# A sparse expert stage whose down matrices are requested by ScalarE instead of SyncE

## The reference, cut to what matters

```
def swiglu(x, w_gu, w_down):
    gate, up = jnp.split(x @ w_gu, 2, axis=-1)
    return (jax.nn.silu(gate) * up) @ w_down
...
    def block(acc, inp):
        tok, wt, ex = inp
        y = swiglu(x_pad[tok], w_gu[ex], w_down[ex])
        return acc.at[tok].add((y * wt[:, None]).astype(acc.dtype)), None
```

## Time and profile before

| | |
|---|---|
| time, median of 3 executions | 2914.94 us (2910.91 to 2915.69) |
| span of the profiled execution | 2949.8 us |
| PE busy | 2637.6 us, 89% of the span |
| DVE, ACT, POOL busy | 762.9, 441.0, 493.7 us |
| expert stage | from about 1941 to 2903 us |
| weight requests of SP in the expert stage | 65 of 2048 KB and 65 of 1024 KB |

### The profile page before, as it was taken

One profiled execution on the slowest core, in us unless ns is written; L12 is line 12 of the kernel. 1 busy time (PEld: TensorE's weight loads), 2 busy tenths in 40 slices (PEclk: granted clock), 3 DMA queues, 4 the chain that ended last, 5 costly groups with the idle time before them and its releaser, 6 DMA issues. The chain is left out here.

```text
span 2949.8 us, 28375 instructions
## 1 busy us (share of the span) xinstructions
PE 2637.6 (89%) x11406; PEld 1618.1 (55%) x11406; DVE 762.9 (26%) x1394; ACT 441.0 (15%) x724; POOL 493.7 (17%) x449
## 2 busy tenths in 40 slices
PE   5999889999997999999994469959999999999992
PEld 3444444346994444444444124447777777778881
DVE  4011544654432111111233202211121211111114
ACT  1001113244541000000000000001111111111110
POOL 2000110111531000000010530012232333322221
PEclk9999999999998999999995779979999999999996
DMA  5011002100003111220104600089989999999984
GB/s 220 29 40 46 15 15 90 43 8 8 1 1 122 32 32 38 58 89 0 71 0 156 127 12 0 0 295 292 273 270 280 282 278 285 291 347 362 356 297 149
DMA packets 179592, 391.58 MB, mean 133 GB/s; under 512 B 14832, under 2 KB 53360, under 8 KB 178704
## 3 DMA queue, kind: packets, MB, share of 16 engines
q1 hardware_dynamic: 153616, 302.67, 30.3%
q0 software_dynamic: 24992, 80.21, 10.9%
q10 hardware_dynamic: 864, 7.02, 0.6%
HBM read 327.48 MB, written 62.39 MB: 132 GB/s over the span
## 5 line engine op out<-in xcount | busy, mean ns | idle before, releaser
L1888 PEld LDWEIGHTS banks<-arena 128*128 128x128 f32 x4160 | 531.3, 191 | 44.3 <-issue 43.1
L1888 PE MATMUL banks<-arena 128*128 128x128 f32 (+7 forms) x4160 | 540.0, 290 | 0.8 <-DVE arena L2046 0.8
L1298 PE MATMUL banks<-arena 128*128 128x512 f32 x768 | 341.0, 596 | 15.9 <-DMA arena<-in_w_branch 12.4
L363 PE MATMUL banks<-arena 128*128 128x512 f32 x640 | 279.2, 593 | 2.2 <-DVE arena L1021 1.9
L1835 POOL DMA_INDIRECT acc_scratch<-arena x100 | 154.5, 1545 | 634.5 <-DMA acc_scratch<-arena 340.5
L1298 PEld LDWEIGHTS banks<-arena 128*128 128x128 f32 x768 | 145.4, 190 | 204.6 <-issue 204.6
L1896 PE MATMUL banks<-arena 128*128 128x512 f32 (+1 forms) x536 | 244.5, 598 | 2.3 <-DVE arena L2048 0.9
L363 PEld LDWEIGHTS banks<-arena 128*128 128x128 f32 x640 | 119.4, 189 | 156.5 <-issue 148.6
L1304 PE MATMUL banks<-arena 128*128 128x512 f32 x384 | 172.7, 592 | 0.0
L356 PE MATMUL banks<-arena 128*128 128x512 f32 x384 | 167.2, 596 | 1.6 <-PEq L282 0.9
L1896 PEld LDWEIGHTS banks<-arena 128*128 128x128 f32 (+1 forms) x536 | 96.1, 189 | 101.8 <-issue 98.1
(11 more groups left out here) (342 smaller groups left out, 2514.8 us busy)
## 6 DMA issues: line engine op xcount, KB each, us to landing
arena<-in_exp_w_gu SPq DMA_DIRECT2D x65, 2048.0 KB
arena<-in_exp_w_down SPq DMA_DIRECT2D x65, 1024.0 KB
arena<-in_w_in SPq DMA_DIRECT2D x10, 2048.0 KB, 9.0
arena<-in_w_in SPq DMA_DIRECT2D x24, 512.0 KB, 5.9
arena<-in_w_branch SPq DMA_DIRECT2D x24, 256.0 KB, 6.1
arena<-in_x SPq DMA_DIRECT2D x4, 1024.0 KB
h_scratch<-arena SPq DMA_DIRECT2D x1, 4096.0 KB, 12.9
arena<-in_w_out SPq DMA_DIRECT2D x2, 2048.0 KB, 12.1
```

Source lines behind the costliest of these rows:

```text
L363: last = nc.tensor.matmul(PS[:, bank, :], wt[:, k, ct * P:(ct + 1) * P], hT[:, k, half * HALF:(half + 1) * HALF], start=(k == 0), stop=(k ...
L1298: last = nc.tensor.matmul(PS[:, b, :], wm[u][:, k, n, :], hT[:, k, hs], start=(k == 0), stop=(k == KD - 1))
L1888: last = nc.tensor.matmul(PS[:, bank + part, f * n:(f + 1) * n], weights[:, k, part * FF + f * P:part * FF + (f + 1) * P], by_k(x, n)[:, k ...
```

## The change

SP no longer requests the down matrices of the ranks. ACT does, in its own queue: four before anything else in the stage, the fifth after the spill loop, and that of rank r+5 at the end of its work on rank r. Each time it first loads the expert's number from the table. The gate/up matrices and the spill expert's two matrices stay with SP.

```
-                    if r >= RING:
-                        sp.wait_ge(x_dn, chunks(r - RING + 1))
-                    sp.dma_start(dn[r % RING], dn_v[bass.ds(e, 1)].rearrange("a p f n -> p (a f) n")).then_inc(x_wd[r % RING], 16)
...
+                def down_in(r):
+                    e = table(act, rank_e, r, NE - 1)
+                    if r >= RING:
+                        act.wait_ge(x_dn, chunks(r - RING + 1))
+                    act.dma_start(dn[r % RING], dn_v[bass.ds(e, 1)].rearrange("a p f n -> p (a f) n")).then_inc(x_wd[r % RING], 16)
+
+                for r in range(RING - 1):
+                    down_in(r)
                 act.wait_ge(x_xt, 1)
                 x_half(0, 0, P)
...
+                act.wait_ge(s_dn, n + 1)
+                act.nop(nofuse=True)
+                down_in(RING - 1)
                 for r in range(NE):
...
                     if more(r):
                         y_half(r, yoB, gateB, more(r), c + 1)
+                    if r + RING < NE:
+                        down_in(r + RING)
```

## The result

| | us |
|---|---|
| before, median of 5 executions | 2914.35 (2910.91 to 2915.69) |
| changed, median of 5 | 2924.63 (2921.76 to 2926.97) |
| ratio | 1.0039, 95% interval 1.0026 to 1.0051 |

The changed kernel is slower by 10.3 us in the medians (11.4 us by the ratio); the interval of the ratio is 7.6 to 14.9 us of 2914. One of the 23 executions of the kernel before on the chip of the last runs took 6534 us, where the others took 2945.5 to 2955.4, and is left out of their ratios.

The account below looks back on a forecast made before the run. PE was taken to bound the expert stage, except its entry, where DMA engines limit. Spill weights +9, scatter and gather -2, the rest 0: +7 us on 2914.94, 2922; own range 2917 to 2926, 8 in 10 2911 to 2933.

Parts of the forecast that it names:

- Steady cost 0: In the ranks: ACT's table load and request, 1.15 us each, hidden in its idle time; 0, bound 0 to 3 us.
- rival 4: ACT is held at its own requests at the entry, delaying its copy of the first rows: +5 to +15 us; chance 0.05.
- rival 3: Two-chunk ranks: a third busy queue lengthens POOL's scatters until its chain bounds the kernel, 25 us, 2940; chance 0.12.
- The delay of the spill weights: Stage entry: four down matrices, 4.19 MB, pass ahead of the spill expert's weights, delaying the spill block's matmuls 9 us.
- the bounds: Stage entry: spill-weight delay depending on how the two queues share, from 3.6 or 6.3 us to the full 10.7 us.
- What comes back: Behind the spill block: scatter and next gather meet an emptied queue and give back 2 us.
- the pair: Spill block's scatter plus the gather behind it: 16.2 us instead of 18.2, bounds 12.8 to 18.2.
- not 5 to 8: Sign in the changed profile: PE's idle for the gather behind the spill block lasts 5 to 8 us, ending near 2000.
- lies beside the scatter: Right after the spill block: rank 4's down request, 1.05 MB, costs 2.7 us at worst, inside 12.8 to 18.2.
- The sum: Whole kernel: +9 - 2 + 0 + 0 = +7 us on 2914.94, giving 2922, range 2917 to 2926.
- The faster one: Entry: small transfers meet an emptied queue and the clock stays up, spill delay under 2 us: 2907; chance 0.08.
- The no-change one: Entry: PE's 8.0 us wait for the gather absorbs a delay of 3.6 to 6 us: 2912 to 2918; chance 0.20.

Follow-up runs that it names:

- the entry undone: Changed kernel, but SP requests ranks 0 to 3's down matrices in their old place; ACT still requests from rank 4 on: 1.0003 of the kernel before.
- the entry alone: Kernel before, but ACT requests the down matrices of ranks 0 to 3 at the stage's start; SP requests all others as before: 1.0011.
- rank 4's request later: Changed kernel, but ACT requests rank 4's down matrix at the end of rank 0, not right behind the spill block: 1.0023 of the kernel before.
- The run in one queue: Kernel before, SP requesting everything, but the down matrices of ranks 0 to 3 ahead of the spill expert's weights: 1.0017.

## Why the prediction was right

- **The bound and the ranks.** "Steady cost 0" held: from rank 1's gate/up to rank 36's output half it is 580.0 us in both first traces and 579.9 to 580.0 in the second of before and with the entry undone. ACT's requests took 0.38 us each, at most 0.43: rival 4 did not occur. POOL's chain (rival 3) did wait longer for its scatters, 349 and 381 us in the two traces of the change against 341 and 313 before, but it did not become the bound. It left one trace on PE, which waits once after 2010 us for a gather, at rank 38, where the two-chunk ranks end; in the changed kernel:

```profile
2564.45 1.09 PE L1878 MATMUL banks<-arena 128*128 128x128 f32 x8 [2.84 <-DMA arena<-hx_scratch,arena]
```

2.8 us instead of 1.4. But the second trace of before has 2.3 us there, so no more than 0.5 to 1.4 us is the change's, if any.

- **The delay of the spill weights.** Forecast 9.0 us; measured 9.55 between the first traces and 8.7 between the second ones. The sharing packet for packet, on which the choice among the bounds rested, is shown by the equal counts above. The Trainium skill, DMA: Bandwidth & Descriptors, section Queues, rings and completion order, says that a DMA engine takes turns between its queues by the packet, and the traces agree (364 to 366 packets). That the four matrices pass in full is also shown without a second queue, in the run with one.

- **What comes back.** This is the step that failed: "I give the pair 18.2 - 2 = 16.2 us". Scatter to rank 1's rows took 20.2 and 19.2 us in the two traces of the change, outside the bounds of 12.8 to 18.2, against 18.2 and 18.6 before. The reasoning behind the 2 us held where it was tried alone, and gave twice as much: with the entry alone, and with rank 4's request later, the pair took 14.3 and 14.0 us, some 4 us less than before. In the change PE sat idle for the gather for 10.0 and 9.0 us, not 5 to 8. (The lower bound of 12.8 contains a shortest gather of 6.4 us that no row shows; the shortest here reached PE in 4.8.) What failed is the sentence that rank 4's down request "lies beside the scatter; 1.05 MB, 2.7 us at worst, inside these bounds". It cost 5 us at rank 1's rows (61.2 to 56.3): 1.7 in the scatter, and 3.5 in the gather, which had lost its head start and met a queue that was no longer empty.

- **The sum.** Forecast +7, 2922 us, with a range of its own of 2917 to 2926; measured +10.3 (7.6 to 14.9), 2924.6 us. By the marks: 9 at the spill block, then 2.0 lost again in the first pair of traces and 0.5 in the second, instead of 2 back, which puts rank 1's rows 10.9 and 8.8 us late. The rest is within the spread of the stage's end. The right sign and place rest on what was shown. That the sum came close is in part luck: some 4 us came back where 2 were forecast, and some 5 were lost where nothing was, and these two nearly cancel.

- **Rivals.** The faster one needed the spill weights to lose under 2 us; they lost 9. The no-change one needed the idle in front of rank 1 to absorb the delay. Half of that occurs (the entry alone, 1.0011), and it is the change's own request that undoes it. The Trainium skill, DMA: Bandwidth & Descriptors, section Issuing engines are not separate DMA queues, says that all issuing engines' transfers run on the same 16 DMA engines. The run in one queue agrees, 26.6 us beside 26.8.

What stays open: the entry undone and the entry alone, 1 and 3 us, sum to less than the change's 10. The table of head starts goes some way. Rank 4's request is in the entry undone too and lengthens the scatter there (11.5 us to the next gather instead of 10.3), but the gather takes 8 us in the kernel before as well, so there is no quick gather to lose; it costs 0.8 us at rank 1's rows beside the second trace of before (1.8 beside the first). Only where the spill block is late and the queue has run empty does it cost 5. The times are less sharp than the marks: three runs have rank 1's rows at 56.3 to 56.6 us and ratios of 1.0011, 1.0017 and 1.0023, on two chips and with overlapping intervals. The rest of the end mark, some 1 to 3 us, is inside the spread of single traces.

## What to carry to other kernels

A request that leaves earlier in a queue of its own is not free: at the start of a stage, where all transfers are wanted at once, each byte that passes ahead of what TensorE needs first delays it, whoever requests it; here by 1.8 to 2.3 us per MB, where 393 GB/s would be 2.5. Order requests by the time of need, and look at the small transfers that a chain depends on: here a gather that met a queue with work, or had less than 1 us of head start on a large request, took 8 to 9 us, and one with an empty queue and 1 us of head start took 5. Where the weights are requested five ranks ahead of their use, moving requests to another engine has nothing to give.

## What the runs showed of the hardware

- A busy queue delays another queue's first packet by more than the turns explain: 4.8 to 5.1 us from request to TensorE in the three traces in which a gather met an empty queue with 1 us of head start, 7.8 to 9.2 us in the eight others of the table, although each queue gets about every second packet once both move.
- 4 KB and 2 KB packets take equal turns, so a queue with the larger packets gets twice the bytes: 1.40 against 0.75 MB in 6 us.
- The same program took 2914 us in its first five executions and 2952 us, 38 us more, in later ones on three chips. The two traces of it have a granted clock of 0.52 and 0.53 from 1700 to 1740 us; the changed kernel, the same up to there, had 1.00 in its first trace and 0.50 in its second, and its times on those occasions were 2924 and 2968 us.
- SP's request for the spill block's down matrix took 0.80 to 1.03 us in the traces in which ACT made whole-matrix requests (4 KB packets) at the same time, and 0.43 us in the two traces of before.
